# Output product, two norms and the residual of a layer as one stage over three sets of tokens

## The chip, the core and the metric

The kernel runs on one core of a Trainium2 chip. The metric is the device time of one launch in microseconds (us). TensorE (PE in the rows; its weight loads stand as PEld) multiplies, VectorE (DVE) and ScalarE (ACT) do element-wise work, SyncE (SP) issues the transfers. SBUF is the working memory of 128 partitions, PSUM holds eight banks of 512 fp32 columns for the results of TensorE.

## The reference

One step of a four-layer hybrid backbone, on 128 context tokens and 1024 latent tokens (1152 together) of width 1024. The layers' token mixers are RWKV-7, attention, a short convolution, and RWKV-7 again. Around each mixer stands the same frame:

```python
def rmsnorm(x, w):
    x32 = x.astype(jnp.float32)
    y = x32 * lax.rsqrt(jnp.mean(x32 * x32, axis=-1, keepdims=True) + RMS_EPS)
    return (y * w.astype(jnp.float32)).astype(x.dtype)

def sublayer(x, cond, p, i, mixer_fn):
    ada = jax.nn.silu(cond) @ p['w_ada'][i] + p['b_ada'][i]
    shift, scale, gate = jnp.split(ada[:, None, :], 3, axis=-1)
    h = rmsnorm(x, p['norm_pre'][i]) * (1.0 + scale) + shift
    m, extra = mixer_fn(h)
    return x + gate * rmsnorm(m, p['norm_post'][i]), extra
```

The last step of every mixer is a product of its gated result `og` (1152 x 1024) with a 1024 x 1024 weight. That product, the norm of its result `m`, the residual sum, and the norm and shift that make the next layer's `h` are the part that this case is about. It occurs four times; after the last layer there is no next norm and `x` is the output.

## The kernel before

Everything is held transposed: a tensor of 1152 tokens by 1024 channels is 8 blocks (NB) of 128 channels, channels on the partitions, tokens along the free axis. `g.x` holds x, `g.arena` is four such tensors (`g.big[0..3]`), each also named as fp32r (`g.big_r`), the number format in which TensorE takes one pass instead of the two records of a plain fp32 product. To keep fp32 accuracy an fp32 product is made of three fp32r products: a high part of both factors, and two with a low part (factor minus its high part).

The program is a chain of phases. Each phase is one block in which every engine runs its own list of instructions, ordered by semaphores, and ends in a barrier of all engines (`Sems.release`, L146). Per layer: `phase_prenorm`, the mixer's phases, `phase_output`; at the end `phase_end` stores x.

`phase_output` (L2233): SP loads the weight in 8 slabs of 128 x 1024 (512 KB) into two slots (`load_slabs`, L346). VectorE splits slab 0 (`split_slab`: cast L380 into `stage_r`, subtraction L391 in place), then the eight row blocks of `og` (`split_rows`: L380, L399), then slab 1. TensorE makes output block b from slab b: for each of 8 row blocks and 3 products, three chunks of 384 tokens, 72 matmuls (`multiply_split`, L412). Two groups of three PSUM banks alternate. ScalarE copies block b to `m` (L2272) and squares it (L2276), VectorE adds the squares up in `acc` (L2297) and splits slab b+2. Only when all eight blocks are there, TensorE sums over the partitions by a product with ones (L2265), VectorE scales and adds epsilon (L2299), ScalarE takes Ln (L2279) and Exp (L2281), and VectorE multiplies `m` by it (L2302) and adds it to x with the gain (L2229), block by block.

`phase_prenorm` (L288), after a barrier: ScalarE squares x (L311), TensorE sums (L283), VectorE L331, ScalarE Ln and Exp (L314, L316), VectorE multiplies x (L334), ScalarE scales and shifts to h (L320). Before the second RWKV layer SP also stores x to DRAM there.

## Time and profile before

| | us |
|---|---|
| median of 3 runs | 5144.27 (5140.68 to 5149.32) |
| the profiled execution | 5141.56 |
| its span, first to last instruction | 5139.8 |
| mean granted TensorE clock over the span | 0.946 of full |
| busy: PE, DVE, ACT | 4371.9 (85%), 2637.6 (51%), 1976.1 (38%) |
| the new stage's place, after layers 0, 1, 2 | 187.0, 186.4, 184.6 |
| the same after layer 3, with the store of y | 161.9 |

The last two lines are measured from the end of the last VectorE instruction of the mixer's last phase (1624.98, 2758.56, 3361.62, 4977.87 us) to the end of the last ScalarE instruction of the next layer's `phase_prenorm` (1811.94, 2944.92, 3546.21), or to the end of the span. The first prenorm, ahead of layer 0, is not touched. A busy time of TensorE counts overlapping matmuls once and says little on its own. What matters in such a chain of phases is in which stretches TensorE has nothing to do.

### The profile page before, as it was taken

How to read it: one execution, taken by the hardware profiler on the slowest of the kernel's cores; microseconds unless marked ns; L12 is line 12 of the kernel's file. 1: busy time of each engine (PE TensorE's matmuls, PEld its weight loads, DVE VectorE, ACT ScalarE, POOL GpSimd, SP SyncE). 2: the span in 40 equal slices, each digit the busy share in tenths (PEclk: the TensorE clock that was granted, in tenths of full speed). 3: DMA queues.
4: the chain of work that ended last, by engine and by line, in shares of the span. 5: the costliest groups of instructions: out<-in, count | busy, mean ns of one | idle time of the engine just before them, and what ended most of it. 6: DMA issues, size and time to landing. Idle time of an engine off the chain costs nothing. (4 is left out here: it accounts for less than half of the span.)

```text
span 5139.8 us, 135171 instructions
## 1 busy us (share of the span) xinstructions
PE 4371.9 (85%) x60324; PEld 3611.7 (70%) x60324; DVE 2637.6 (51%) x4169; ACT 1976.1 (38%) x3418; POOL 2.7 (0%) x8
## 2 busy tenths in 40 slices
PE   3799988999987689888888599985999989999966
PEld 0488867888874655446667499983888777888846
DVE  0552447777764313145565343336533477777753
ACT  1553225555544223046663300015432245555441
POOL 0000000000000000000000000000000000000000
PEclk7899999999998889989999799997999989999988
DMA  9134593333316010000000011111345843333261
GB/s 417 49 112 128 156 257 114 92 95 93 93 55 164 17 40 29 27 1 1 1 1 26 17 37 45 41 33 62 102 130 157 236 139 94 95 92 90 65 164 57
DMA packets 624902, 465.61 MB, mean 91 GB/s; under 512 B 27488, under 2 KB 600288, under 8 KB 619744
## 3 DMA queue, kind: packets, MB, share of 16 engines
q1 hardware_dynamic: 493536, 391.29, 24.9%
q10 hardware_dynamic: 130816, 66.07, 4.7%
q8 instruction: 458, 7.50, 0.6%
q14 instruction: 92, 0.75, 0.1%
HBM read 333.28 MB, written 123.99 MB: 89 GB/s over the span
## 5 line engine op out<-in xcount | busy, mean ns | idle before, releaser
L412 PE MATMUL ps<-big_r,stage_r 128*128 128x384 f32 x3072 | 625.6, 338 | 86.0 <-DVE big_r L399 85.7
L660 PE MATMUL ps<-big_r,stage_r 128*128 128x384 f32 x2976 | 640.6, 350 | 17.1 <-DVE big_r L891 15.8
L412 PEld LDWEIGHTS ps<-big_r,stage_r 128*128 128x128 f32 x3072 | 545.9, 190 | 94.5 <-issue 85.7
L660 PEld LDWEIGHTS ps<-big_r,stage_r 128*128 128x128 f32 x2976 | 521.8, 189 | 101.2 <-issue 53.6
L412 PE MATMUL ps<-big_r,w_slab_r 128*128 128x384 f32 x1536 | 351.9, 337 | 0.0
L660 PE MATMUL ps<-big_r,w_slab_r 128*128 128x384 f32 x1488 | 340.3, 336 | 0.0
L368 PE MATMUL ps<-arena,w_slab 128*128 128x384 f32 x864 | 295.0, 503 | 27.0 <-DVE arena L1953 24.1
L412 PEld LDWEIGHTS ps<-big_r,w_slab_r 128*128 128x128 f32 x1536 | 277.1, 190 | 0.0
L368 PEld LDWEIGHTS ps<-arena,w_slab 128*128 128x128 f32 x864 | 169.2, 197 | 153.2 <-issue 47.5
L2105 DVE TENSOR_REDUCE extra<-ps 128x1 f32<-128x1152 f32 (+1 forms) x144 | 171.8, 1234 | 200.3 <-PE ps L2017 200.3
L660 PEld LDWEIGHTS ps<-big_r,w_slab_r 128*128 128x128 f32 x1488 | 268.1, 189 | 0.0
L1434 ACT COPY arena<-ps 128x512 f32<-128x512 f32 x288 | 169.1, 587 | 256.7 <-PE ps L1239 256.1
L1588 DVE COPY_PREDICATED arena<-arena,ps 128x128 f32<-128x128 uint32 x720 | 192.9, 325 | 118.6 <-PE ps L1227 117.6
L2085 ACT COPY arena<-ps 128x384 f32<-128x384 f32 (+1 forms) x400 | 175.3, 470 | 197.1 <-PE ps L2035 197.0
L1461 ACT COPY arena<-ps 128x256 f32<-128x256 f32 x360 | 136.5, 379 | 275.9 <-PE ps L1250 225.2
L2035 PE MATMUL ps<-ident,arena 128*128 128x128 f32 x1168 | 189.7, 287 | 51.2 <-DVE arena L2118 23.8
L768 ACT ACTIVATE x_resid<-ps,chan 128x384 f32<-128x384 f32 x192 | 101.2, 579 | 305.6 <-PE ps L694 242.3
L380 DVE CAST stage_r<-w_slab 128x1024 fp32r<-128x1024 f32 x64 | 44.4, 694 | 339.1 <-DMA w_slab<-in_w 328.0
L1227 PE MATMUL ps<-arena 64*64 64x32 f32 x7680 | 166.7, 222 | 57.2 <-ACT arena L1434 49.0
L1239 PE MATMUL ps<-arena 64*64 64x64 f32 x9216 | 202.9, 224 | 9.5 <-issue 5.6
L1192 PE MATMUL ps<-arena 64*128 64x128 f32 x2304 | 172.6, 289 | 43.1 <-DVE arena L1560 29.9
L2035 PEld LDWEIGHTS ps<-ident,arena 128*128 128x128 f32 x1168 | 123.3, 141 | 106.1 <-DVE arena L2112 80.6
(221 smaller groups left out, 7677.4 us busy)
## 6 DMA issues: line engine op xcount, KB each, us to landing
w_slab<-in_w SPq DMA_DIRECT2D x138, 512.0 KB, 3.7
scan_in<-x_resid ACTq DMA_DIRECT2D x112, 576.0 KB, 5.4
arena<-in_w_ada SPq DMA_DIRECT2D x24, 2048.0 KB, 27.6
arena<-scan_in SPq DMA_DIRECT2D x80, 576.0 KB, 7.6
arena<-scan_in SPq DMA_DIRECT2D x144, 320.0 KB, 3.9
arena<-scan_in SPq DMA_DIRECT2D x288, 128.0 KB, 3.9
arena<-scan_in SPq DMA_DIRECT2D x144, 192.0 KB, 4.2
scan_y<-arena SPq DMA_DIRECT2D x144, 128.0 KB, 2.2
```

The lines of the kernel that those rows point to most:

```text
L368: mm = pe.matmul(g.ps[:, bank + c, 0:CW], g.slab[:, slot, k * P:(k + 1) * P], rhs[:, k, c * CW:(c + 1) * CW], start=k == 0, stop=k == NB - 1)
L412: mm = pe.matmul(g.ps[:, bank + c, 0:CW], w[:, k * P:(k + 1) * P], x[:, k, c * CW:(c + 1) * CW], start=k == i == 0, stop=k == NB - 1 and i ...
L660: mm = pe.matmul(g.ps[:, 3 * s + c, 0:CW], w[:, k * P:(k + 1) * P], x[:, k, chunk(c)], start=k == i == 0, stop=k == NB - 1 and i == 2)
L1192: mm = pe.matmul(strided(ps, (3 + h) * 512 + u * P, (1, P)), strided(bk[q % 2], u * 256 + t * P, (1, P), rows=HALVES[h]), strided(ar[q % 4 ...
L1227: mm = pe.matmul(strided(ps, p * 512 + u * 32, (1, 32), rows=HALVES[h]), strided(gr[q % 3], (1 - p) * 1024 + h * 512 + u * P, (1, HD), row ...
L1239: mm = pe.matmul(strided(ps, h * 512 + (2 * d + s) * HD, (1, HD), rows=HALVES[p]), strided(xt[q % 2], lx(d, p, s), (1, HD), rows=HALVES[h] ...
L1434: A.copy(strided(x, 0, (HD, 2), (P, 4), (1, HD)), strided(ps, 0, (512, 2), (HD, 4), (1, HD))).then_inc(xa_ok, 1)
L1461: A.copy(strided(xt[q % 2], n, (256 - n, 2), (2 * n, P // n), (1, n)), src).then_inc(xt_ok, 1)
L1588: V.copy_predicated(strided(wk(k), p * P, (256 + n, 2), (2 * n, HD // n), (1, n)), bits(strided(level_mask, (k - 1) * P, (HD, 2), (n, HD / ...
L2035: mm = pe.transpose(g.ps[:, turned_bank(n, h, k), i * P:(i + 1) * P], prob[n % 2][h][:, (3 * k + i) * P:(3 * k + i + 1) * P], g.ident[:, :])
L2085: A.copy(prob_t[n % 2][h][:, 3 * k * P:3 * k * P + w], g.ps[:, turned_bank(n, h, k), 0:w]).then_inc(tr_ok, 1)
L2105: V.tensor_reduce(nmax[n % 2][h], scored(n, h), mybir.AxisListType.X, ALU.max, negate=True).then_inc(max_ok, 1)
```

## The change

`phase_output`, the following `phase_prenorm` and `phase_end` become one phase, `phase_boundary`. The tokens are taken in three sets of 512, 384 and 256 (`CHUNKS`). A unit (i, b) is output block b for set i: 8 row blocks by 3 products, 24 matmuls as wide as the set, into one of six PSUM banks in turn. Banks 6 and 7 hold the sums of the two norms. The weight's high and low parts are kept for all eight slabs (`w_high`, `w_low`, in the arena), so each slab is loaded and split once, during set 0; ScalarE now casts the high part (`high_slab_of`), VectorE makes the low part (`low_slab_of`). Row blocks are split set by set (`split_row`, order in `ROWS_AT`). What follows a set's last unit, called its tail here, is issued while TensorE works on the next set: `sum1`, `mean1`, `root1` (Ln, Exp) for the norm of m, `residual`, then `square2`, `add2`, `sum2`, `mean2`, `root2` for the norm of x, then `scaled` (VectorE) and `shifted` (ScalarE). `RESIDUAL_AT`, `SQUARE_AT` and `RESULT_AT` say beside which unit of the next set each is issued. The tail of set 2 has nothing beside it. `sq1`, `acc1`, `rstd1` lie in `stage`, `acc2`, `rstd2` in `extra`, `sq2` in `w_slab`. After the last layer the second norm is left out and y is stored set by set; so is x ahead of the second RWKV layer. The convolution's buffers are renumbered so that h is where the stage leaves it, with no other change there.

```diff
+        phase_prenorm(nc, g, layers[0])
         for layer in layers:
             j = layer // 3
-            phase_prenorm(nc, g, layer)
...
-            phase_output(nc, g, layer)
-        phase_end(nc, g)
+            phase_boundary(nc, g, layer, layer == layers[-1])
...
+CHUNKS = ((0, 512), (512, 896), (896, 1152))
+ROWS_AT = ((0, 1, 2), (3,), (), (), (4, 5), (6,), (7,), ())
+RESIDUAL_AT = ((), (0,), (1, 2, 3), (4, 5, 6), (7,), (), (), ())
+SQUARE_AT = ((), (), (0, 1, 2), (3, 4, 5), (6,), (7,), (), ())
+RESULT_AT = ((), (), (0,), (1, 2, 3), (4,), (5,), (6,), (7,))
...
+            for b in range(NB):
+                if b >= WSLOTS:
+                    sp.wait_ge(wl_ok, b - WSLOTS + 1)
+                sp.dma_start(g.slab[:, b % WSLOTS, :], g.io["w"][base + b]).then_inc(slab_in[b % WSLOTS], 16)
+            dest = g.io["y"] if last else g.x_kept[1] if MIXER[layer + 1] == 0 else None
+            if dest is not None:
+                for i in range(LAST + 1):
+                    sp.wait_ge(x_ok, NB * (i + 1))
+                    sp.dma_start(dest[:, :, tokens(i)], g.x[:, :, tokens(i)]).then_inc(x_st, 16)
+                sp.wait_ge(x_st, 16 * (LAST + 1))
...
+            def unit(i, b):
+                u = NB * i + b
+                if i == 0:
+                    pe.wait_ge(wl_ok, b + 1)
+                if u >= 6:
+                    pe.wait_ge(m_ok, u - 5)
+                for k in range(NB):
+                    if b == 0:
+                        pe.wait_ge(row_ok, NB * i + k + 1)
+                    for j, (w, r) in enumerate(((w_high, highs[i % 2][:, k, 0:wide[i]]), (w_high, og_r[:, k, tokens(i)]),
+                                                (w_low, highs[i % 2][:, k, 0:wide[i]]))):
+                        mm = pe.matmul(g.ps[:, bank(i, b), 0:wide[i]], w[:, b, k * P:(k + 1) * P], r,
+                                       start=k == j == 0, stop=k == NB - 1 and j == 2)
+                mm.then_inc(unit_mm, 1)
...
+            def sum2(i):
+                pe.wait_ge(acc2_ok, added(i, NB - 1))
+                if i:
+                    pe.wait_ge(ms2_ok, i)
+                pe.matmul(g.ps[:, 7, 0:wide[i]], g.ones[:, :], part(acc2, i), start=True, stop=True).then_inc(sum2_mm, 1)
+
+            for i in range(LAST + 1):
+                for b in range(NB):
+                    unit(i, b)
+                    if i and b == 0:
+                        sum1(i - 1)
+                    if i and b == 6 and not last:
+                        sum2(i - 1)
...
+            def square1(i, b):
+                u = NB * i + b
+                act.wait_ge(unit_mm, u + 1)
...
+            def result(i, b):
+                if i:
+                    act.wait_ge(x_ok, NB * (i - 1) + b + 1)
+                A.copy(part(m[b], i), g.ps[:, bank(i, b), 0:wide[i]]).then_inc(m_ok, 1)
...
+            high_slab_of(0)
+            high_slab_of(1)
...
+            for i in range(LAST + 1):
+                for b in range(NB):
+                    square1(i, b)
+                    if i == 0:
+                        result(i, b)
+                        if b + 2 < NB:
+                            high_slab_of(b + 2)
+                        continue
+                    for k in RESULT_AT[b]:
+                        result(i, k)
+                    if b == 0:
+                        root1(i - 1)
+                    if last:
+                        continue
+                    for k in SQUARE_AT[b]:
+                        square2(i - 1, k)
+                    if b == 6:
+                        root2(i - 1)
+                    if b == 7 and i < LAST:
+                        for k in range(NB):
+                            shifted(i - 1, k)
+            root1(LAST)
+            if not last:
+                for b in range(NB):
+                    square2(LAST, b)
+                    shifted(LAST - 1, b)
+                root2(LAST)
+                for b in range(NB):
+                    shifted(LAST, b)
...
+            def residual(i, b):
+                if b == 0:
+                    dve.wait_ge(rstd1_ok, i + 1)
+                dve.wait_ge(m_ok, NB * i + b + 1)
+                for c, a0, a1 in pieces(i):
+                    V.scalar_tensor_tensor(part(m[b], i, a0, a1), part(m[b], i, a0, a1), gain(b, c), part(rstd1, i, a0, a1),
+                                           op0=ALU.mult, op1=ALU.mult).then_inc(t_ok, 1)
+                dve.wait_ge(t_ok, t_count(i, b))
+                V.tensor_tensor(g.x[:, b, tokens(i)], part(m[b], i), g.x[:, b, tokens(i)], op=ALU.add).then_inc(x_ok, 1)
...
+            split_row(0, 0)
+            low_slab_of(0)
+            for k in range(1, NB):
+                split_row(0, k)
+            low_slab_of(1)
+            for i in range(LAST + 1):
+                for b in range(NB):
+                    add1(i, b)
+                    if i == 0 and b + 2 < NB:
+                        low_slab_of(b + 2)
+                    if i and b == 0:
+                        mean1(i - 1)
+                    if i < LAST:
+                        for k in ROWS_AT[b]:
+                            split_row(i + 1, k)
+                    if i:
+                        for k in RESIDUAL_AT[b]:
+                            residual(i - 1, k)
+                            if k and not last:
+                                add2(i - 1, k - 1)
+                        if b == 5 and not last:
+                            add2(i - 1, NB - 1)
+                        if b == 6 and not last:
+                            mean2(i - 1)
+                        if b == 7 and i < LAST and not last:
+                            for k in range(NB):
+                                scaled(i - 1, k)
+            mean1(LAST)
+            if not last:
+                for b in range(NB):
+                    scaled(LAST - 1, b)
             for b in range(NB):
-                if b + 2 < NB:
-                    split_slab(nc, g, dve, b + 2, slab_in, proj_done, high_ok, low_ok)
-                dve.wait_ge(sq_ok, b + 1)
-                if b:
-                    dve.wait_ge(acc_ok, b)
-                V.tensor_tensor(acc, acc, sq[b % 2], op=ALU.add).then_inc(acc_ok, 1)
-            dve.wait_ge(sum_mm, 1)
-            V.tensor_scalar(as3(ms), slot_view(g.ps[:, 0:3, :]), 1.0 / D, RMS_EPS, ALU.mult, ALU.add).then_inc(ms_ok, 1)
-            dve.wait_ge(rstd_ok, 1)
-            for b in range(NB):
-                V.tensor_tensor(tmp[:, b, :], m[:, b, :], rstd, op=ALU.mult).then_inc(tmp_ok, 1)
-                if b:
-                    dve.wait_ge(tmp_ok, b)
-                    residual(nc, g, ada, tmp, b - 1, x_ok)
-            dve.wait_ge(tmp_ok, NB)
-            residual(nc, g, ada, tmp, NB - 1, x_ok)
-            dve.wait_ge(x_ok, 2 * NB)
-
-
-def phase_end(nc, g):
-    with ExitStack() as ctx:
-        stored = Sems(nc, ctx)("stored_y")
-        block = ctx.enter_context(nc.Block())
-
-        @block.sync
-        def _(sp):
-            sp.dma_start(g.io["y"], g.x[:, :, :]).then_inc(stored, 16)
-            sp.wait_ge(stored, 16)
-
+                residual(LAST, b)
+            if not last:
+                mean2(LAST)
+                for b in range(NB):
+                    scaled(LAST, b)
```

VectorE, layer 0, the end of the stage. Before, after the last sum of squares the whole width of 1152 tokens is treated at once, and x is written with the gain in one instruction per token group:

```order
L391 TENSOR_TENSOR w_slab_r<-w_slab,stage_r 128x1024
L2297 TENSOR_TENSOR arena<-arena 128x1152 x3
L2299 TENSOR_SCALAR arena<-ps 128x1152
L2302 TENSOR_TENSOR arena<-arena 128x1152 x2
L2229 SCALAR_TENSOR_TENSOR x_resid<-arena,ada,x_resid 128x128
L2229 SCALAR_TENSOR_TENSOR x_resid<-arena,ada,x_resid 128x1024
```

Now, from set 0's `mean2` (L2484) on, at the end of set 1 and the start of set 2: L2450 is `add1`, L2489 `scaled` of set 0, L2454 `mean1` of set 1, L2461 and L2464 the two steps of `residual` of set 1, L2477 `add2`:

```order
L2484 TENSOR_SCALAR extra<-ps 128x512
L2450 TENSOR_TENSOR stage<-stage 128x384
L2489 TENSOR_TENSOR arena<-x_resid,extra 128x512 x8
L2454 TENSOR_SCALAR stage<-ps 128x384
L2450 TENSOR_TENSOR stage<-stage 128x256
L2461 SCALAR_TENSOR_TENSOR arena<-arena,ada,stage 128x384
L2464 TENSOR_TENSOR x_resid<-arena,x_resid 128x384
L2450 TENSOR_TENSOR stage<-stage 128x256
L2461 SCALAR_TENSOR_TENSOR arena<-arena,ada,stage 128x384
L2464 TENSOR_TENSOR x_resid<-arena,x_resid 128x384
```

The tail's instructions of one set have moved between the `add1` of the next. On ScalarE the same place, before, was the end of the stage:

```order
L2272 COPY arena<-ps 128x1152
L2276 ACTIVATE arena<-arena 128x1152
L2279 ACT_TABLE_LOAD
L2279 ACTIVATE arena<-arena 128x1152
L2281 ACT_TABLE_LOAD
L2281 ACTIVATE arena<-arena 128x1152
```

Now, from the last `shifted` of set 0 (L2389) on: L2355 is `square1` of set 2, L2364 and L2366 `root1` of set 1, L2360 `result`, L2378 `square2` of set 1:

```order
L2389 ACTIVATE arena<-arena,ada 128x128
L2389 ACTIVATE arena<-arena,ada 128x384
L2355 ACTIVATE stage<-ps 128x256
L2364 ACT_TABLE_LOAD
L2364 ACTIVATE stage<-stage 128x384
L2366 ACT_TABLE_LOAD
L2366 ACTIVATE stage<-stage 128x384
L2355 ACTIVATE stage<-ps 128x256 x2
L2360 COPY arena<-ps 128x256
L2378 ACTIVATE w_slab<-x_resid 128x384 x3
```

The eight `shifted` of set 0 stand ahead of the first square of set 2, and the function tables of Ln and Exp are loaded in the middle of the sets, ten times a stage where there were four.

## Rows read from the trace of the kernel before

**Rows 1.** Windows: length, busy PE, PEld, DVE, ACT, POOL; clock; DMA share; GB/s.
```profile
1624.98:1634.24 9.26, 0.00 (x0) 0.03 (x1) 4.09 (x6) 0.00 (x0) 0.00 (x0) 0.50 0.32 114
1634.24:1738.16 103.92, 103.58 (x576) 102.30 (x576) 37.40 (x36) 16.02 (x14) 0.00 (x0) 0.97 0.10 31
1738.16:1811.94 73.78, 21.95 (x54) 11.83 (x54) 36.22 (x35) 33.49 (x34) 0.00 (x0) 0.67 0.00 0
2758.56:2944.92 186.36, 125.60 (x630) 114.22 (x630) 77.73 (x76) 49.52 (x48) 0.00 (x0) 0.84 0.07 23
3361.62:3546.21 184.59, 123.04 (x630) 112.26 (x630) 77.70 (x76) 49.52 (x48) 0.00 (x0) 0.84 0.13 49
4977.87:5139.80 161.93, 107.11 (x582) 103.83 (x582) 66.12 (x67) 23.20 (x20) 0.00 (x0) 0.83 0.15 55
```

**Rows 2.** Timeline, VectorE, layer 0: first slab cast; a run of eight like instructions.
```profile
1630.08 0.69 DVE L380 CAST stage_r<-w_slab 128x1024 fp32r<-128x1024 f32 x1 [5.10 <-DMA w_slab<-in_w]
...
1798.30 10.24 DVE L334 TENSOR_TENSOR arena<-x_resid,arena 128x1152 f32<-128x1152 f32 x8 [3.70 <-ACT arena L316]
```

**Rows 3.** Timeline, TensorE, layer 0 (start, us, what, count).
```profile
1637.26 2.12 PE L412 MATMUL ps<-big_r,stage_r 128*128 128x384 f32 x6
1639.18 1.03 PE L412 MATMUL ps<-big_r,w_slab_r 128*128 128x384 f32 x3
...
1700.52 1.20 PE L412 MATMUL ps<-big_r,stage_r 128*128 128x384 f32 x6
1701.56 0.68 PE L412 MATMUL ps<-big_r,w_slab_r 128*128 128x384 f32 x3
```

**Rows 4.** Groups by line and form, ScalarE (count, busy us, mean ns).
```profile
L1461 ACT COPY arena<-ps 128x256 f32<-128x256 f32 x360 | 136.5, 379 | 275.9 <-PE ps L1250 225.2 <-PE ps L1260 50.3
L1430 ACT ACTIVATE arena<-arena 128x512 f32<-128x512 f32 x144 | 82.9, 626 | 0.0
L320 ACT ACTIVATE arena<-arena,ada 128x1024 f32<-128x1024 f32 x32 | 39.2, 1226 | 0.0
L320 ACT ACTIVATE arena<-arena,ada 128x128 f32<-128x128 f32 x32 | 15.4, 481 | 5.7 <-DVE arena L334 5.7
L779 ACT CAST stage_r<-w_slab 128x1024 fp32r<-128x1024 f32 x12 | 12.6, 1046 | 18.0 <-DMA w_slab<-in_w 16.0 <-ACT x_resid L739 2.0
L2279 ACT ACT_TABLE_LOAD x4 | 5.1, 1283 | 0.1
```

**Rows 5.** Groups by line and form, VectorE.
```profile
L391 DVE TENSOR_TENSOR w_slab_r<-w_slab,stage_r 128x1024 fp32r<-128x1024 f32 x64 | 78.5, 1226 | 2.2
L1539 DVE TENSOR_TENSOR arena<-arena 128x512 f32<-128x512 f32 x72 | 49.3, 685 | 0.0
L380 DVE CAST stage_r<-w_slab 128x1024 fp32r<-128x1024 f32 x64 | 44.4, 694 | 339.1 <-DMA w_slab<-in_w 328.0 <-issue 11.1
L2229 DVE SCALAR_TENSOR_TENSOR x_resid<-arena,ada,x_resid 128x1024 f32<-128x1024 f32 x32 | 40.9, 1279 | 0.0
L1612 DVE TENSOR_TENSOR arena<-arena 128x256 f32<-128x256 f32 x72 | 30.6, 425 | 2.5
L380 DVE CAST big_r<-arena 128x1152 fp32r<-128x1152 f32 x40 | 30.1, 753 | 0.0
L2229 DVE SCALAR_TENSOR_TENSOR x_resid<-arena,ada,x_resid 128x128 f32<-128x128 f32 x32 | 11.1, 346 | 0.0
```

**Rows 6.** Timeline, TensorE, attention's phase: plain fp32 products of 256 and 512 columns.
```profile
1829.82 22.61 PE L1862 MATMUL ps<-arena 128*128 128x256 f32 x104
...
1890.24 1.88 PE L1885 MATMUL ps<-arena,extra 128*128 128x512 f32 x4
```

**Rows 7.** Issues of transfers on the page, and the last one's time in the timeline.
```profile
scan_in<-x_resid ACTq DMA_DIRECT2D x112, 576.0 KB, 5.4
...
out_y<-x_resid SPq DMA_DIRECT2D x1, 4608.0 KB, 12.5
...
5126.49 0.35 SPq L2318 DMA_DIRECT2D out_y<-x_resid  x1
```

More of the change, by code:

```diff
@@ L2241, in phase_output @@
-    sq = [work[:, i, :] for i in range(2)]
-    acc = work[:, 5, :]
-    ms, root, rstd = work[:, 2, :], work[:, 3, :], work[:, 4, :]
-    ada = g.ada[:, layer]
-    V, A = nc.vector, nc.scalar
+    n = NB * T
+    w_at, rest_at = (n if og_at == 0 else 0), 3 * n
+    w_high, w_low = g.w_out[w_at]
+    wide = [a1 - a0 for a0, a1 in CHUNKS]
+    at, highs = rest_at, []
+    for k in range(2):
+        size = max(wide[k::2])
+        highs.append(g.big_r[3][:, :, :].rearrange("p b t -> p (b t)")[:, at - rest_at:at - rest_at + NB * size].rearrange("p (b t) -> p b t", b=NB))
+        at += NB * size
@@ new lines, in phase_boundary @@
+    halves = (w_at + 2 * NB * D, at)
+    assert at + 4 * 512 <= 4 * n
+    m = [g.arena[:, halves[b // 4] + b % 4 * 512:halves[b // 4] + (b % 4 + 1) * 512] for b in range(NB)]
+    flat = g.stage[:, :, :].rearrange("p a b -> p (a b)")
+    sq1 = [flat[:, 512 * i:512 * i + 512] for i in range(2)]
+    acc1, rstd1 = flat[:, 1024:1536], flat[:, 1536:2048]
+    acc2, rstd2 = g.extra[:, 0:512], g.extra[:, 512:1024]
+    sq2 = [g.slab[:, i, 0:512] for i in range(2)]
+    gain = lambda b, c: g.ada[:, layer, 16 + b, c:c + 1]
@@ new lines, in phase_boundary, with pieces, part @@
+    V, A = nc.vector, nc.scalar
+    LAST = len(CHUNKS) - 1
+    def pieces(i):
+        return [(c, max(r0, CHUNKS[i][0]), min(r1, CHUNKS[i][1])) for c, r0, r1 in token_ranges()
+                if max(r0, CHUNKS[i][0]) < min(r1, CHUNKS[i][1])]
+    def part(ap, i, a0=None, a1=None):
+        start = CHUNKS[i][0]
+        return ap[:, 0:wide[i]] if a0 is None else ap[:, a0 - start:a1 - start]
+    tokens = lambda i: slice(*CHUNKS[i])
+    t_count = lambda i, b: sum(NB * len(pieces(k)) for k in range(i)) + (b + 1) * len(pieces(i))
@@ new lines, in sum1 @@
+            def sum1(i):
+                pe.wait_ge(acc1_ok, added(i, NB - 1))
+                if i:
+                    pe.wait_ge(ms1_ok, i)
+                pe.matmul(g.ps[:, 6, 0:wide[i]], g.ones[:, :], part(acc1, i), start=True, stop=True).then_inc(sum1_mm, 1)
+            def sum2(i):
[3 more added lines that the diff above has]
+                pe.matmul(g.ps[:, 7, 0:wide[i]], g.ones[:, :], part(acc2, i), start=True, stop=True).then_inc(sum2_mm, 1)
@@ new lines, in _ @@
+            for i in range(LAST + 1):
[5 more added lines that the diff above has]
+                        sum2(i - 1)
+            sum1(LAST)
+            if not last:
+                pe.wait_ge(ms2_ok, LAST)
+                for b in range(NB):
+                    pe.wait_ge(sq2_ok, NB * LAST + b + 1)
+                    pe.matmul(g.ps[:, 7, 0:wide[LAST]], g.ones[:, :], part(sq2[b % 2], LAST), start=b == 0, stop=b == NB - 1).then_inc(last_mm, 1)
@@ L2280, in _, with high_slab_of @@
-            act.wait_ge(root_ok, 1)
-            A.activation(rstd, root, ACT.Exp, scale=-0.5).then_inc(rstd_ok, 1)
+            def high_slab_of(b):
+                act.wait_ge(slab_in[b % WSLOTS], 16 * (b // WSLOTS + 1))
+                A.copy(w_high[:, b, :], g.slab[:, b % WSLOTS, :]).then_inc(wh_ok, 1)
+            def square1(i, b):
+                u = NB * i + b
+                act.wait_ge(unit_mm, u + 1)
+                if b >= 2:
+                    act.wait_ge(acc1_ok, added(i, max(b - 2, 1)))
+                elif i:
+                    act.wait_ge(acc1_ok, added(i - 1, b + NB - 2))
+                A.activation(part(sq1[b % 2], i), g.ps[:, bank(i, b), 0:wide[i]], ACT.Square).then_inc(sq1_ok, 1)
@@ new lines, in result, with root1 @@
+            def result(i, b):
+                if i:
+                    act.wait_ge(x_ok, NB * (i - 1) + b + 1)
+                A.copy(part(m[b], i), g.ps[:, bank(i, b), 0:wide[i]]).then_inc(m_ok, 1)
+            def root1(i):
+                act.wait_ge(ms1_ok, i + 1)
+                A.activation(part(rstd1, i), part(rstd1, i), ACT.Ln).then_inc(ln1_ok, 1)
+                act.wait_ge(ln1_ok, i + 1)
+                A.activation(part(rstd1, i), part(rstd1, i), ACT.Exp, scale=-0.5).then_inc(rstd1_ok, 1)
@@ new lines, in add2 @@
+            def add2(i, b):
+                dve.wait_ge(sq2_ok, NB * i + b + 1)
+                if b == 0:
+                    return
+                if b == 1:
+                    if i:
+                        dve.wait_ge(sum2_mm, i)
+                    first = part(sq2[0], i)
+                else:
+                    dve.wait_ge(acc2_ok, added(i, b - 1))
+                    first = part(acc2, i)
+                V.tensor_tensor(part(acc2, i), first, part(sq2[b % 2], i), op=ALU.add).then_inc(acc2_ok, 1)
```

116 lines of the change are left out of this document (80 added, 36 removed).

## The prediction

> **What bounds the kernel now.** I read the windows first, because the change touches four places of a long chain of phases. Around layer 0's output product the window has three parts [rows 1]: 9.3 us in which TensorE does nothing, 103.9 us of products at 0.97 of the clock, and 73.8 us in which TensorE has 54 short matmuls, while VectorE (36 us) and ScalarE (33 us) take turns. So the product itself is bound by TensorE, and 83 of 187 us are not covered by it. The places after layers 1 and 2 are alike (186.4 and 184.6 us), the last is 161.9 us long and ends with the store of y [rows 1]. The four are 720 us of 5141.56; the rest of the kernel is the same code, and I count it as unchanged.
>
> **What stays.** The number of matmuls stays (8 x 72 = 3 x 8 x 24 = 576), and so do the columns. At full clock six 384-wide fp32r matmuls take 1.04 us, 0.1733 each, that is 384/2.4 = 160 ns and 13 more [rows 3]; at half clock 1.92/6 = 0.320 [rows 3]. No row shows 512 or 256 wide in fp32r. The plain fp32 products bound them from below: 256 columns take 22.61/104 = 0.217 us a record, 512 about 0.43, and such a record passes its columns at half the rate, so 0.108 and 0.215 for a single pass [rows 6]. From above, 256 can cost what 384 does, 0.173, if the weight load sets the pace (the loads stand beside every matmul, busy 102.3 us of the 103.9 [rows 1]), and 512 adds its 13 ns: 0.227. I take column time plus 13 ns: 0.2267, 0.1733, 0.120, since 384 is the nearest row; it is near the lower bound for 256. Units are then 5.44, 4.16 and 2.88 us, 99.8 us for all 24, as 8 x 72 x 0.1733 before.
>
> **A rule on the other side.** The Trainium skill, "TensorE: Matmul & The Clock Gate", section "LDWEIGHTS (loading the stationary operand)", gives a load by its column count alone, 128/1.2 = 107 ns, which would fit under 256 columns and leave no loss. Its section "Back-to-back issue gap" gives N/2.4 + 2.5 ns. The trace disagrees for fp32r: 173 ns, not 162.5, at 384 wide. By that gap the set 0 and set 2 units would be 5.2 and 2.6 us. The sum below uses neither.
>
> **Other durations.** VectorE, fp32, by line through the forms: a sum or product of 512, 384, 256 columns 0.685, 0.555, 0.425; gain times norm (as L2229) of 128, 384, 256: 0.346, 0.61, 0.48; cast of 512 0.46 [rows 5]. ScalarE: square, copy, Ln or Exp 0.38 at 256, some 0.48 at 384, 0.6 at 512; scale and shift 0.48, 0.59, 0.69 at 128, 256, 384; cast of a slab 1.05; a function table 1.28 [rows 4]. Like instructions overlap: eight of 1.353 take 10.24, so about 0.09 less each [rows 2]; a dependent one starts about 0.03 late. This is an estimate for each new width.
>
> **A middle stage, from the end of the mixer.** Set 0: slab 0 is there at 5.1 as before [rows 2]. Row block 0 is split while it flies. Cast on ScalarE 1.05 and low part on VectorE 1.23 give the first matmul at 7.4 (9.3 before). Seven more row blocks at 0.46 + 0.69 less overlap, 1.09 each, reach 15.1, and unit 0 ends at 15.8; TensorE, at half clock for its first 5 to 6 us [rows 1, 3], needs 1.28 per row block there and then catches up. Low slab 1 comes at 16.3. Seven units of 5.44: 54.4. Slab b+2 is ready 0.6 + 0.6 + 1.05 + 1.23 = 3.5 after unit b, hidden under unit b+1 (5.4); with less than 3.5 of cover it would show each time.
>
> Set 1: 8 x 4.16 and two sums over 512 columns in plain fp32, 0.86 each. TensorE reaches `sum2(0)` at 84.2. VectorE has rstd1 at 62.5 and starts `residual(0, 0)` at 65.3; the first takes 1.5, seven blocks of residual and `add2` 2.09 each (14.6), six `add1` 2.8, three row blocks 2.1, waits for the squares 0.8: 87.1. So TensorE waits 2.9 us, and set 1 ends at 92.3.
>
> Set 2: TensorE has its seven units and `sum1(1)` done at 112.9. ScalarE squares and copies unit 7 (93.1), waits for `scaled`, and shifts all of set 0: 8 x (0.39 + 0.60), to 102.0. Queued behind stand the first square of set 2 and `root1(1)` with two table loads: 105.6. On that waits VectorE: from 106.3 eight residuals of 1.1, seven `add2` of 0.47, the `add1` of 0.34 between, to 119.9. `sum2(1)` sits ahead of unit 7 on TensorE, which waits 7.0 us. Then 0.64 and 2.88: 123.6.
>
> Tail of set 2, nothing beside it: square, add, sum, mean 2; eight `scaled` of set 1, 4; eight residuals of 0.85, 6.8, with the squares and ScalarE's `shifted` of set 1 (0.93 a block) ending at 137.7; mean, Ln, table, Exp to 140.8; first `scaled` 0.5, eight shifts of 0.5 to 145.4. The savings are 187.0, 186.4 and 184.6 less 145.4: 41.6, 41.0 and 39.2. The two barriers inside are in them.
>
> **The last stage** has no second norm, so nothing waits: 54.4 + 33.3 + 0.86 = 88.5, + 23.0 + 0.64 = 112.2. Square to Exp 3.9, eight residuals 6.9: 123.0. The store is 1 MB instead of 4.5. Between 576 KB at 5.4 and 4608 KB at 12.5 that is 6.2 us; 0.8 follows as before (5126.49 + 12.5 against 5139.8) [rows 7]. 130.0 against 161.9: 31.9 saved. The store of x before layer 3, 1 MB again, is hidden under mean, root and shifts (9 us); the loads of the next phase wait for the barrier as now.
>
> Sum: 41.6 + 41.0 + 39.2 + 31.9 = 153.7. The profiled execution goes from 5141.56 to 4987.9. The median is 2.7 above the profiled one; I forecast the median, 4990.
>
> **The rivals.** (1) 256-wide matmuls at the weight load's pace, 0.173: unit 4.16 in set 2. In a middle stage six of the units are under the 7 us wait and one shows with some rest, +3.2; in the last +10.2. Together +19.8: 5010. For it: the loads stand as dense as the matmuls. Against: at half clock 384 takes 0.320, no more than its columns, so loads didn't bind there. 0.13. (2) The 7 us wait lets the clock fall: in the window behind the product the granted clock is 0.67 [rows 1]. Unit 7 of set 2 then costs 24 x 0.213 = 5.1 instead of 2.9, the sums behind it double; +3.5 a stage, +10: 5000. 0.13. (3) No 13 ns at other widths, 0.215 and 0.108: 2.1 less in a middle stage, 3.3 in the last, 9.5 in all: 4981. This is the time that the skill's gap rule named above would give. 0.08. (4) The change doesn't do what it says: the in-order queues put each tail on TensorE's path. Sets 0 and 1 have some 20 us of tail each, so a middle stage would be back at 185 and only the last one gain: 5110. Against: 7 us, not 20, is what I find. 0.04. (5) Slower: TensorE's stops keep the granted clock at half through the sets. Then 576 matmuls take 192 x (0.427 + 0.320 + 0.213) = 184 instead of 99.8, four times +84.5 = 338, and 5144 - 154 + 338 = 5328. It decides from 154/338 = 45% of the columns at half. Against: before, with row blocks coming one by one, half clock lasted 5 to 6 us and the window has 0.97 [rows 1]; set 0 has no stop after its first unit. 0.02.
>
> **How the numbers follow.** The forecast has 0.60 and, with 2 to 4 us of error a stage from the widths without a row, its own range is 4976 to 5004. The range that leaves out less than 2 in 10 goes from rival 3 less that error, 4970, to rival 1 plus some of it, 5018. A difference of 0.2% (10 us) is what a measurement of this kernel can tell from none. Faster 0.97, same 0.01, slower 0.02.
>
> **What would show it.** First matmul 7.4 us after the mixer, unit 0's end at 16. Matmul starts 227, 173, 120 ns apart. TensorE idle for about 3 us ahead of `sum2` in set 1, released by `add2`, and 7 us in set 2; none in the last stage. ScalarE in one piece of 8 us of `shifted` at the start of set 2. 22 us from the last unit to the last shift. The middle stages 145, the last 130. Wrong would be: 173 ns at 256 wide; a granted clock of half inside the sets; unit ends of set 0 more than 5.5 us apart, which would mean the slab path is not hidden; or other phases that change their length.

## The result, and the profile after

The changed kernel takes 5010.66 us (median of 4 runs, 5006.82 to 5015.15), the kernel before, beside it, 5146.55 (5140.68 to 5149.32): a ratio of 0.9738, 95% interval 0.9721 to 0.9755. Forecast were 4990 and a range of 4970 to 5018, so the range holds it and the forecast is 20.7 us too low. The profiled execution took 5006.82 us with a span of 5005.0.

The four places, windows as in [rows 1] (the columns are the same):

```profile
1634.03:1784.60 150.57, 118.30 (x602) 102.44 (x602) 89.92 (x178) 77.38 (x136) 0.00 (x0) 0.86 0.09 29
2730.46:2880.21 149.75, 118.46 (x602) 102.69 (x602) 89.94 (x178) 77.38 (x136) 0.00 (x0) 0.88 0.09 29
3295.99:3444.75 148.76, 117.08 (x602) 102.17 (x602) 89.92 (x177) 77.39 (x136) 0.00 (x0) 0.89 0.18 61
4876.75:5005.00 128.25, 105.31 (x582) 95.06 (x582) 69.78 (x136) 39.41 (x68) 0.00 (x0) 0.90 0.20 70
```

150.6, 149.8, 148.8 and 128.3 us stand against 187.0, 186.4, 184.6 and 161.9 before: 36.4, 36.6, 35.8 and 33.6 saved, 142.4 in all, where the forecast had 153.7. The rest of the span, which the change leaves alone, is 4427.7 us against 4420.0. Layer 0's stage cut into its sets, by windows again:

```profile
1634.03:1650.00 15.97, 8.32 (x24) 5.72 (x24) 10.63 (x19) 2.11 (x3) 0.00 (x0) 0.63 0.29 99
1650.00:1688.50 38.50, 38.39 (x169) 31.81 (x170) 18.20 (x29) 13.17 (x20) 0.00 (x0) 1.00 0.22 69
1688.50:1728.10 39.60, 36.84 (x198) 35.00 (x198) 26.17 (x56) 19.20 (x33) 0.00 (x0) 0.96 0.00 0
1728.10:1762.50 34.40, 27.11 (x196) 25.82 (x194) 20.57 (x40) 24.03 (x48) 0.00 (x0) 0.85 0.01 1
1762.50:1784.60 22.10, 7.65 (x18) 4.08 (x18) 14.35 (x35) 18.87 (x34) 0.00 (x0) 0.64 0.00 0
```

Set 0 behind its first unit is TensorE alone: 38.39 of 38.50 us, 169 matmuls, 0.228 each. VectorE works 26 us and ScalarE 19 in set 1, where before they had 36 and 33 us behind the product [rows 1]. So the tails are covered. But set 2 has 7.3 us without TensorE and a granted clock of 0.85. TensorE's timeline shows where (start, us, line, what, first shape, count; in brackets the idle time ahead and what ended it; a row can run over from one unit's shape to the next's):

```profile
1641.53 8.41 PE L2312 MATMUL ps<-big_r,w_out 128*128 128x512 f32 x24 [15.14 <-DVE w_out L2429]
1650.11 42.57 PE L2312 MATMUL ps<-big_r,w_out 128*128 128x512 f32 x192 [0.17 <-DVE w_out L2429]
...
1721.27 2.07 PE L2326 MATMUL ps<-extra,ones 128*128 128x512 f32 x2 [2.77 <-DVE extra L2477]
1722.35 8.55 PE L2312 MATMUL ps<-big_r,w_out 128*128 128x384 f32 x48
1730.75 0.81 PE L2320 MATMUL ps<-stage,ones 128*128 128x384 f32 x2
1731.10 17.72 PE L2312 MATMUL ps<-big_r,w_out 128*128 128x256 f32 x144
1756.11 1.65 PE L2326 MATMUL ps<-extra,ones 128*128 128x384 f32 x2 [7.29 <-DVE extra L2477]
1756.98 5.52 PE L2312 MATMUL ps<-big_r,w_out 128*128 128x256 f32 x24
1763.43 0.70 PE L2320 MATMUL ps<-stage,ones 128*128 128x256 f32 x2 [0.94 <-DVE stage L2450]
```

L2326 is `sum2`. Both waits stand where the prediction put them, 2.77 and 7.29 us long (2.9 and 7.0 forecast), and both are ended by `add2` (L2477). What the prediction had not taken into its sum is behind them, in windows of TensorE (length, busy and count, clock, DMA share, GB/s):

```profile
1718.50:1721.30 2.80, 0.04 (x2) 0.94 0.00 0
1721.30:1724.30 3.00, 3.00 (x6) 0.50 0.00 0
1724.30:1727.70 3.40, 3.40 (x21) 0.99 0.00 0
...
1748.80:1756.10 7.30, 0.02 (x1) 0.70 0.01 2
1756.10:1762.20 6.10, 6.09 (x25) 0.52 0.01 3
```

Behind the 2.8 us stop the granted clock is 0.50, the 1.2 GHz level, for about 3 us; behind the 7.3 us stop it is 0.52 over all of unit (2, 7). That unit's 24 matmuls take 5.52 us in the timeline. At full clock they take 3.32 (below). In layer 2 the half clock ended inside that unit, whose first and last starts are 4.23 us apart instead of 5.24; this is why the stage there is 1.0 us shorter than in layer 1.

### The profile page after: what moved, and what is told of

Read it like the earlier page. It is cut to its first block and busy times, and to the rows that moved or that the text cites. A ratio compares the mean times of both kernels' runs of the same rounds, so it can differ in the third digit from the quotient of the medians.

```text
span 5005.0 us, 135676 instructions
## 1 busy us (share of the span) xinstructions
PE 4352.7 (87%) x60240; PEld 3573.9 (71%) x60240; DVE 2677.8 (54%) x4545; ACT 2075.3 (41%) x3730; POOL 2.7 (0%) x8
## 5 line engine op out<-in xcount | busy, mean ns | idle before, releaser
L663 PE MATMUL ps<-big_r,stage_r 128*128 128x384 f32 x2976 | 642.8, 351 | 16.9 <-DVE big_r L894 15.5
L663 PEld LDWEIGHTS ps<-big_r,stage_r 128*128 128x128 f32 x2976 | 524.0, 190 | 100.9 <-issue 54.1
L2312 PE MATMUL ps<-big_r,w_out 128*128 128x512 f32 (+2 forms) x2304 | 428.6, 348 | 47.8 <-DVE w_out L2429 47.6
L2312 PEld LDWEIGHTS ps<-big_r,w_out 128*128 128x128 f32 x2304 | 385.0, 196 | 92.8 <-DVE w_out L2429 51.1
L663 PE MATMUL ps<-big_r,w_slab_r 128*128 128x384 f32 x1488 | 340.9, 336 | 0.0
L415 PE MATMUL ps<-big_r,stage_r 128*128 128x384 f32 x1536 | 309.1, 335 | 17.1 <-DVE big_r L402 17.0
L415 PEld LDWEIGHTS ps<-big_r,stage_r 128*128 128x128 f32 x1536 | 270.5, 188 | 19.1 <-issue 16.6
L663 PEld LDWEIGHTS ps<-big_r,w_slab_r 128*128 128x128 f32 x1488 | 268.5, 189 | 0.0
L2038 PEld LDWEIGHTS ps<-ident,arena 128*128 128x128 f32 x1168 | 123.6, 141 | 105.9 <-DVE arena L2115 80.3
L1195 PEld LDWEIGHTS ps<-arena 64*128 64x128 f32 x2304 | 144.8, 192 | 73.1 <-issue 47.8
```

The costliest lines, as they stand in the source:

```text
L415: mm = pe.matmul(g.ps[:, bank + c, 0:CW], w[:, k * P:(k + 1) * P], x[:, k, c * CW:(c + 1) * CW], start=k == i == 0, stop=k == NB - 1 and i ...
L663: mm = pe.matmul(g.ps[:, 3 * s + c, 0:CW], w[:, k * P:(k + 1) * P], x[:, k, chunk(c)], start=k == i == 0, stop=k == NB - 1 and i == 2)
L1195: mm = pe.matmul(strided(ps, (3 + h) * 512 + u * P, (1, P)), strided(bk[q % 2], u * 256 + t * P, (1, P), rows=HALVES[h]), strided(ar[q % 4 ...
L2038: mm = pe.transpose(g.ps[:, turned_bank(n, h, k), i * P:(i + 1) * P], prob[n % 2][h][:, (3 * k + i) * P:(3 * k + i + 1) * P], g.ident[:, :])
L2312: mm = pe.matmul(g.ps[:, bank(i, b), 0:wide[i]], w[:, b, k * P:(k + 1) * P], r, start=k == j == 0, stop=k == NB - 1 and j == 2)
```

## The experiments

Each kernel is the changed one with one edit. "Stage" is measured as in the table of before, in the profiled execution; "outside" is the span less the four stages.

| kernel | median us | ratio to before (95%) | middle stages | last | outside |
|---|---|---|---|---|---|
| before | 5146.55 | | 187.0, 186.4, 184.6 | 161.9 | 4420.0 |
| the change | 5010.66 | 0.9738 (0.9721 to 0.9755) | 150.6, 149.8, 148.8 | 128.3 | 4427.7 |
| before again | 5146.61 | 0.9998 (0.9988 to 1.0008) | 186.9, 186.2, 187.3 | 161.3 | 4424.5 |
| the change again | 5016.68 | 0.9732 (0.9706 to 0.9758) | 150.7, 149.8, 148.7 | 128.4 | 4432.0 |
| busy_wait | 4997.65 | 0.9698 (0.9676 to 0.972) | 146.4, 145.8, 145.9 | 128.6 | 4426.4 |
| sum2_late | 5000.82 | 0.9705 (0.9686 to 0.9725) | 147.9, 146.9, 147.1 | 128.5 | 4421.3 |
| shift_spread | 4998.05 | 0.9694 (0.9673 to 0.9715) | 144.2, 145.1, 143.3 | 128.4 | 4437.9 |
| serial_tails | 5188.12 | 1.0077 (1.0055 to 1.01) | 199.7, 199.0, 198.5 | 164.8 | 4420.9 |
| equal_sets | 4977.8 | 0.9665 (0.9647 to 0.9683) | 140.0, 139.3, 138.8 | 132.8 | 4425.9 |
| sets_448 | 4975.77 | 0.9667 (0.965 to 0.9683) | 140.9, 140.5, 140.3 | 128.3 | 4424.1 |
| equal_middle | 4974.41 | 0.9656 (0.9642 to 0.9669) | 139.9, 139.2, 138.8 | 129.1 | 4433.7 |
| equal_spread | 4971.43 | 0.9661 (0.9648 to 0.9675) | 140.4, 139.7, 139.9 | 128.4 | 4419.7 |

The ratio is that of the runs taken side by side. The stages of the change hardly move between its two executions (150.6 and 150.7), one place of before moves by 2.7 us (184.6 and 187.3), and the outside moves by up to 18 us over the twelve.

**The change again.** The same kernel, to see what repeats.

> The changed kernel once more, unedited: how far the phases that the change doesn't touch move from one execution to the next. Theory A (the 7.8 us that the changed kernel's execution has outside the four new stages, most of it before the first of them, is spread between executions): the stages come again at 150.6, 149.8, 148.8 and 128.3 us within 1, the phases ahead of the first one at 1634.0 within 10 us either way, by the clock that is granted there. Rival (the new program slows the other phases): 1634 within 1 us again, and the total 5007 to 5015.

The stages came back within 0.2 us each. The first began at 1631.6 instead of 1634.0, more than the 1 us that the rival allows, and the outside was 4.3 us longer. So the stages of the change are solid, the saving in them is 142 us (144 against the second execution of before, further down), and the kernel's time carries some us of spread that has nothing to do with them.

**Waits filled with products (busy_wait).** My theory is that the missing 5 us a middle stage are the clock behind the two waits. The rival is that the chain of VectorE and ScalarE is longer than I worked out. The edit puts products ahead of both `sum2`, as many as the wait is long, whose results `sum2` overwrites:

```diff
+            def busy(i, n):
+                if i:
+                    pe.wait_ge(ms2_ok, i)
+                for _ in range(n):
+                    pe.matmul(g.ps[:, 7, 0:256], w_high[:, 0, 0:P], highs[1][:, 0, 0:256] if i == 0 else highs[0][:, 0, 0:256], start=True, stop=True)
...
             def sum2(i):
+                busy(i, (20, 56)[i])
                 pe.wait_ge(acc2_ok, added(i, NB - 1))
```

> Ahead of each sum2 TensorE is kept at work by products of 256 columns into the free bank 7, 20 in set 1 and 56 in set 2 (2.4 and 6.7 us, inside the waits of 2.9 and 7.4). Theory (the 5 us that a middle stage took over the forecast are the clock's, lost behind the two waits): the unit behind each wait runs at full clock, 4.2 and 2.9 us in place of 5.4 and 5.3, and a middle stage falls from 150 to about 146; 12 us in all, ratio to the changed kernel 0.9976. Rival (they are late VectorE and ScalarE work, and the clock costs nothing because TensorE is not what ends the stage): a middle stage stays at 150.

TensorE's timeline of busy_wait (L2326 are the added products, L2333 is `sum2`) and two of its windows:

```profile
1712.49 2.55 PE L2326 MATMUL ps<-big_r,w_out 128*128 128x256 f32 x20
1715.43 1.13 PE L2333 MATMUL ps<-extra,ones 128*128 128x512 f32 x2 [0.40 <-DVE extra L2484]
1715.99 7.60 PE L2312 MATMUL ps<-big_r,w_out 128*128 128x384 f32 x48
...
1741.34 6.88 PE L2326 MATMUL ps<-big_r,w_out 128*128 128x256 f32 x56
1748.81 0.91 PE L2333 MATMUL ps<-extra,ones 128*128 128x384 f32 x2 [0.59 <-DVE extra L2484]
1749.26 3.32 PE L2312 MATMUL ps<-big_r,w_out 128*128 128x256 f32 x24
```

```profile
1716.00:1718.50 2.50, 2.50 (x15) 1.00 0.00 0
...
1748.80:1752.40 3.60, 3.59 (x26) 1.00 0.00 0
```

76 products more and a stage 4.1, 4.0 and 2.8 us shorter (4 each were expected). The clock stays at 1.00, the last unit takes 3.32 instead of 5.52 and the sums half. The stop in set 1 is part of it: unit (1, 7) has its last start 92.12 us after the mixer instead of 93.68, and `sum2(1)` comes at 120.54 instead of 122.08.

The first matmul doesn't fall alike in all stages (7.50, 6.53 and 6.62 us after the mixer in the change). Counted from it, the three stages of busy_wait are 139.0 us each, those of the change 143.1, 143.2 and 142.1, and the forecast of 145.4 less 7.4 is 138.0. So the clock theory stands, with 4.1, 4.2 and 3.1 us, and 1.0 is left in each stage for the other engines.

**The second sum behind unit 7 (sum2_late).** This asks what sets the end once TensorE isn't held back: with `sum2` behind unit 7, TensorE does the unit first and waits after it.

```diff
-                    if i and b == 6 and not last:
+                    if i and b == 7 and not last:
                         sum2(i - 1)
```

> sum2 of the set before is issued behind unit 7 in place of behind unit 6. TensorE no longer waits in set 1 (unit 7 ends at 88.5, not 93.7) and in set 2 waits only when its products are done. Theory (the end of a middle stage is set by the chain of ScalarE and VectorE, the place of sum2 on TensorE matters only through the clock): a middle stage 145 to 147, since no unit runs at half clock behind a wait; the last stage unchanged at 128.3. Rival (TensorE's place of the wait is the bound): set 2 ends 9 us earlier and the stage falls by nearly as much, to 141 to 142.

The stages are 147.9, 146.9 and 147.1, near the 145 to 147 of the chain theory and far from 141 to 142. `sum2(1)` now stands alone, with the last unit done ahead of it:

```profile
1748.02 1.65 PE L2326 MATMUL ps<-extra,ones 128*128 128x384 f32 x2 [5.15 <-DVE extra L2477]
```

It starts at 120.79 us, about where busy_wait has it (120.54). The end hangs on when VectorE has its sums, whichever side of it the last unit stands. So the 7 us wait was not there to be won on TensorE.

**The shifts spread out (shift_spread).** Which link of the chain in set 2 can be shortened? ScalarE's block of shifts stands at its start, ahead of `root1(1)`; in the changed kernel, its timeline:

```profile
1729.80 7.99 ACT L2389 ACTIVATE arena<-arena,ada 128x128 f32<-128x128 f32 x16 [0.86 <-DVE arena L2489]
1737.69 0.36 ACT L2355 ACTIVATE stage<-ps 128x256 f32<-128x256 f32 x1
1738.07 1.28 ACT L2364 ACT_TABLE_LOAD   x1
```

The edit issues one row block's shift behind each unit of set 2 instead:

```diff
-                    if b == 7 and i < LAST:
-                        for k in range(NB):
-                            shifted(i - 1, k)
+                    if i == LAST and b:
+                        shifted(0, b - 1)
+                    if i == LAST and b == 7:
+                        shifted(0, 7)
```

> The eight shifted of set 0, one block of 8 us on ScalarE ahead of set 2's first square, are issued one behind each unit of set 2. Theory (that block is what makes sum2 of set 1 late): root1 of set 1 comes 8 us earlier, TensorE's wait in set 2 falls from 7.4 to 3 to 4 us, a middle stage to 147 to 148. Rival (the chain from residual to add2 on VectorE is the bound by its own length): the wait falls by less than 1 us and the stage stays at 150.

```profile
1722.25 1.13 PE L2326 MATMUL ps<-extra,ones 128*128 128x512 f32 x2 [2.78 <-DVE extra L2478]
...
1751.37 1.65 PE L2326 MATMUL ps<-extra,ones 128*128 128x384 f32 x2 [3.04 <-DVE extra L2478]
1752.24 4.39 PE L2312 MATMUL ps<-big_r,w_out 128*128 128x256 f32 x24
```

In layer 0 `sum2(1)` comes at 116.25 instead of 122.08, 5.8 us earlier, and the stages are 6.4, 4.7 and 5.4 us shorter, more than expected. Not all of that is the shifts'. In layers 0 and 2 the clock stayed at 1.00 behind the first stop (2.78 us), where it fell in the changed kernel (windows at the end of this text); unit (1, 7) has its last start at 92.09, as in busy_wait. In layer 1 it fell as in the changed kernel:

```profile
2809.45 2.07 PE L2326 MATMUL ps<-extra,ones 128*128 128x512 f32 x2 [2.78 <-DVE extra L2478]
2810.53 8.65 PE L2312 MATMUL ps<-big_r,w_out 128*128 128x384 f32 x48
```

Counted from the first matmul, `sum2(1)` is 4.2 us earlier there and 5.7 and 5.8 in the other two, so 4.2 us are the shifts' and the other 1.5 the clock's. The wait fell to 3.04, as expected, but the root came only 6.5 us earlier in layer 0, not 8, because its Ln now waits for VectorE's mean:

```profile
1733.99 0.52 ACT L2364 ACTIVATE stage<-stage 128x384 f32<-128x384 f32 x1 [1.85 <-DVE stage L2455]
```

The outside was the longest of all in that execution, 4437.9, which hides part of the gain in the span. So the head of the chain, ScalarE's 8 us, was on the path.

**Before again.** The kernel before as a kernel of its own, to see how far the outside moves by itself.

> The kernel before once more, unedited, for the spread of the phases outside the four places. Three executions of the new kernels have reached the first of the four between 1627.2 and 1635.1 us, the one of before at 1625.0. Theory A (spread between executions, most of it in the scan): before comes anywhere in 1624 to 1636, and its four places again at 187.0, 186.4, 184.6 and 161.9 within 1. Rival (the new program is slower there): again 1625 within 1.

Ratio 0.9998, and an outside of 4424.5 against 4420.0. The first place begins at 1626.7, which fits theory A and is only 0.7 us outside what the rival allows, so this run alone doesn't decide between them. Its last middle stage is 187.3 here and 184.6 in the profiled execution of before: [rows 1] is at the short end there by up to 3 us.

**The tails in series (serial_tails).** All that the change does but one thing: each set's tail is finished before the next set's products. The edit moves calls and makes TensorE wait for the end of each tail (the two `wait_ge`); TensorE's part of it:

```diff
                 for b in range(NB):
                     unit(i, b)
-                    if i and b == 0:
-                        sum1(i - 1)
-                    if i and b == 6 and not last:
-                        sum2(i - 1)
+                if i < LAST:
+                    sum1(i)
+                    if last:
+                        pe.wait_ge(x_ok, NB * (i + 1))
+                    else:
+                        sum2(i)
+                        pe.wait_ge(h_ok, t_count(i, NB - 1))
```

> The same stage, sets, slabs and instructions, but each set's tail is done before TensorE begins the next set, so that the gain of laying them beside it is taken away alone. Theory (the gain is the cover of the tails; the merged phase without it gives none): tails of 38, 29 and 21 us stand in the open, starts of sets 1 and 2 at half clock cost 2 to 3 each, a middle stage is about 204, the last about 166, the whole 5205, slower than before. Rival (the gain comes from the barriers gone, the slabs resident and the first unit's earlier start): it stays faster than before, under 5120.

```profile
1684.49 1.13 PE L2320 MATMUL ps<-stage,ones 128*128 128x512 f32 x2 [1.41 <-DVE stage L2445]
1705.67 2.08 PE L2326 MATMUL ps<-extra,ones 128*128 128x512 f32 x2 [20.05 <-DVE extra L2472]
1719.86 20.44 PE L2312 MATMUL ps<-big_r,w_out 128*128 128x384 f32 x101 [12.12 <-ACT arena L2392]
```

199 us a middle stage, longer than the 187 of before, and 5188.12 us (two executions): 0.8% slower than before. Three sets without cover cost some 13 us a stage (204 was expected); the cover gives 49 back (199.7 less 150.6), its higher granted clock included (0.86 over the stage against 0.78). The last stage is 164.8, 2.9 longer than before. TensorE stands still for 20.05 and 12.12 us in one tail, where the changed kernel has 2.77. Without the overlap nothing of the gain is left.

**Three sets of 384 (equal_sets).** The 7 us wait is there because the tail of 384 tokens has only 256 tokens' products to hide under. With equal sets each has the same cover, and only the bare tail at the end grows.

```diff
-CHUNKS = ((0, 512), (512, 896), (896, 1152))
+CHUNKS = ((0, 384), (384, 768), (768, 1152))
```

> Three sets of 384. The work of set 0's tail on VectorE and ScalarE shrinks by a quarter, and set 2 gives 33 us of cover for the tail of set 1 in place of 23. Theory (the queues of VectorE and ScalarE in sets 1 and 2 are what makes TensorE wait): waits ahead of sum2 under 1 us in both sets, no half clock behind them, the open tail of set 2 longer by 3.5 us; a middle stage 139 to 141, the last stage 130 to 131 in place of 128.3: 4978 to 4985 where the changed kernel gives 5007 to 5015. Rival (the sizes matter little, the chain has its length whatever they are): the waits come back in the longer tail, a middle stage 147 to 150.

```profile
1699.41 0.91 PE L2326 MATMUL ps<-extra,ones 128*128 128x384 f32 x2 [0.56 <-DVE extra L2477]
1699.86 8.78 PE L2312 MATMUL ps<-big_r,w_out 128*128 128x384 f32 x48
...
1734.09 0.81 PE L2326 MATMUL ps<-extra,ones 128*128 128x384 f32 x2
1734.44 4.62 PE L2312 MATMUL ps<-big_r,w_out 128*128 128x384 f32 x24
```

The waits are 0.56 us and none, the clock behind them is full, and the middle stages are 9.9 to 10.6 us shorter than the changed kernel's. The last one is 4.5 longer, 132.8 where 130 to 131 was expected: nothing waits there in either, and the last set with its store is bigger. Counted from the first matmul, which came 0.7 us later here, it is 3.8 longer.

**Sizes between (sets_448).** 448, 384 and 320 in the middle stages, with the shifts spread, and 512, 384, 256 in the last. Beside the line shown, the edit is that of shift_spread.

```diff
+    CHUNKS = ((0, 512), (512, 896), (896, 1152)) if last else ((0, 448), (448, 832), (832, 1152))
```

> Middle stages by sets of 448, 384 and 320 with set 0's shifted one behind each unit of set 2; the last stage with the sizes of the change, 512, 384, 256, for which nothing waits there. By the same durations a middle stage is 139 to 141 and the last 128.3, 4975 to 4982, ratio to before about 0.967; if the sizes matter little it equals the kernel with shifted alone spread, 144.

140.9, 140.5, 140.3 and 128.3, as expected: the last stage as it was, the middle ones 0.9 to 1.4 us over equal sets. TensorE's wait in set 1 is 1.66 us here, with the clock at 1.00 behind it, and there is none in set 2.

**The best sizes for each stage (equal_middle), and the same with the shifts spread (equal_spread).** The line shown is the whole edit of the first; the second adds that of shift_spread.

```diff
+    CHUNKS = ((0, 512), (512, 896), (896, 1152)) if last else ((0, 384), (384, 768), (768, 1152))
```

> Three sets of 384 in the three middle stages, 512, 384 and 256 in the last. The stages are independent of each other, so each should keep the length that it had where its sets were alike: middle 139 to 140 us (equal sets showed 139.99, 139.31, 138.84), last 128.3 to 128.5 (it was 132.81 with equal sets, whose last store is larger). Against equal sets in all four places that is 4.4 us less: 4970 to 4976. If the sizes of the last stage don't matter, it stays at 4977.8.

> As equal_middle, and the shifts of set 0 stand one behind each unit of set 2 instead of all eight ahead of it. The theory that the shifts matter only because sum2(1) waits for the chain behind them expects little here, since with equal sets sum2(1) is reached only about when it is ready: 138 to 140 us a middle stage, at most 1.5 us less than equal_middle. The rival, that the shifts also hold back ScalarE's part of the tail after the last unit, expects 3 us or more a stage, as with 512, 384 and 256, where the spread was worth 5 to 6.5.

139.9, 139.2 and 138.8 for the first, as expected; its last stage, 129.1, is 0.6 us over the 128.3 to 128.5 expected, because the first matmul came at 7.40 us instead of 6.60. With equal sets the spread buys nothing (140.4, 139.7, 139.9, up to 1.1 us longer), where it gave 4.7 to 6.4 with falling sizes, the clock's part included: the block of shifts cost something only through the wait of `sum2(1)`. The three last kernels can't be told apart by their times (4971 to 4976, with intervals that overlap), nor from equal_sets at 4977.8; all are 33 to 39 us under the change.

## Why the prediction was right, and what it missed

**The structure was right.** In layer 0: first matmul 7.50 us after the mixer (7.4 forecast), the last start of unit (0, 0) at 15.51 (end 15.8), that of set 0 at 54.08 (end 54.4), `sum2(0)` at 87.24 (87.1), the shifts of set 0 one piece of 7.99 us (8), a wait of 7.29 (7.0). In layers 1 and 2 the first matmul came at 6.53 and 6.62, which one sum for all three stages had missed. Serial_tails shows that rival (4), tails on TensorE's path, would have given 199 a stage, worse than its 185, and that it isn't what happens here. Rival (5), half clock through the sets, falls with 1.00 in set 0.

**The widths were right.** From one start to the next the matmuls stand 0.227, 0.173 and 0.120 us apart (medians over a unit), the values chosen for 512, 384 and 256. So rival (1), 0.173 at 256 wide, and rival (3), no 13 ns at the other widths, both fall. The last stage, which has no second norm, shows the sum of them with nothing in between: the last unit has its last start 111.1 us after the mixer, where its end was forecast at 112.2. Counted from the first matmul, at 6.60 instead of 7.4, the difference is 0.2. `sum1(2)` follows at 112.3 (4989.06 less 4876.75), when VectorE has its sum.

```profile
4967.53 20.60 PE L2312 MATMUL ps<-big_r,w_out 128*128 128x256 f32 x168
4989.06 0.70 PE L2320 MATMUL ps<-stage,ones 128*128 128x256 f32 x2 [0.94 <-DVE stage L2450]
```

The Trainium skill, "TensorE: Matmul & The Clock Gate", section "Back-to-back issue gap", gives N/2.4 + 2.5 ns for the gap of a matmul by itself: 216, 163 and 109 ns. The trace has 11 ns more at each of the three widths, in fp32r.

**The mis-sized term: the clock behind the waits.** The step is "`sum2(1)` sits ahead of unit 7 on TensorE, which waits 7.0 us. Then 0.64 and 2.88: 123.6." The 2.88 is a unit at full clock; it ran at half, in layer 2 for its first part. Rival (2) had named this with +3.5 a stage and 0.13, and the sum had left it out, though the window behind the product of before, with its 0.67 [rows 1], spoke for it. Rival (2) also applied it to the long wait only. The wait of 2.77 us in set 1 cost as well: unit (1, 7) has its last start at 93.68, against an end of 92.3 forecast. Through the square of that unit, VectorE's `scaled`, ScalarE's queue and `root1(1)` this lateness reaches `sum2(1)`.

Busy_wait, where the clock stays full, splits the 5.2 us between the forecast 145.4 and the 150.6 of layer 0:

- 1.5 from the clock behind the stop in set 1 (`sum2(1)` at 122.08 against 120.54).
- 2.6 from the clock behind the stop in set 2 (from the start of `sum2(1)` to the last start of unit (2, 7) 6.11 us against 3.49).
- 0.6 from the chain to `sum2(1)` (120.54 against 119.9). Most of it stands in ScalarE's queue: in busy_wait the shifts end at 102.2 (102.0 forecast) and `root1(1)`, behind a square and two table loads, at 106.2 (105.6). (A middle stage has twelve table loads, not the ten named with the change.)
- 0.6 from the tail of set 2, 22.4 us in both kernels behind the last start, 21.8 allowed.
- Less 0.2, since the recorded 119.9 + 0.64 + 2.88 is 123.4 and not 123.6.

The other sums of the prediction come out within 0.2 us a term, but for rival (3): by its own spacings the last stage is 4.3 us less, not 3.3, which changes nothing.

**The last stage** was forecast at 130.0 and took 128.3. The products were 1.0 us earlier than forecast and the way from them to the last residual 0.6 longer, so the residuals end at 122.6 (123.0). The store is issued at 4999.39, 5.6 us ahead of the end of the span, where 6.2 + 0.8 = 7.0 had been allowed.

**The rest of the kernel.** "The rest of the kernel is the same code, and I count it as unchanged": it came out 7.7 us longer in the profiled execution. Over the twelve profiled executions it lies between 4419.7 and 4437.9 us, and the kernels with the changed stage are at both ends of that. Most of it arises ahead of the first changed line: the first stage begins between 1625.0 and 1636.9 us, its scan phase takes 782.7 to 795.7 us with the same instructions. Both executions of before are at the low end (1625.0 and 1626.7), those of the change at 1634.0 and 1631.6, but equal_spread and equal_sets, whose code up to there is that of the change, start at 1625.2. I take it for spread between executions. What causes it stays open.

**The sum again.** The profiled execution was to take 4987.9 and took 5006.82, 18.9 more: 11.3 are stages (153.7 less 142.4) and 7.7 the unchanged phases. The median lies 3.8 above the profiled execution instead of 2.7, and 0.6 went in rounding 4990.6 to 4990; that is the 20.7. With rival (2) as the forecast it would have been 5000, and the stage 148.9.

**That the range held is partly luck.** 5010.66 lies outside the 4976 to 5004 that the prediction gives its own forecast. It lies inside 4970 to 5018, whose upper end was set by rival (1), and the 0.120 us at 256 columns refutes that rival. What moved the result was the clock of rival (2), priced at 3.5 us a stage and worth 4.1, 4.2 and 3.1, and the unchanged phases, which no rival had.

**What the change left.** The profile of a covered tail says what to size: the tail of a set must fit under the products of the next set. Falling sizes give the smallest bare tail at the end (22.4 us behind the last unit) and the least cover for the tail before it. In layer 0 equal sets have the last start of the last unit 113.5 us after the mixer instead of 128.2 and 26.5 us of bare tail behind it, 4.1 more, so they are better in the three stages with both norms; in the last, where the second norm is missing, nothing waits, and the small last set is better.

## What to carry to other kernels

When work is taken in sets so that the element-wise tail of one hides under the products of the next, work out for each pair whether the tail fits, and choose the sizes by that before making the last set small. Price a wait of TensorE as the wait plus what comes behind it: here 7 us of waiting cost 2.6 us more in the sum and the 24 matmuls behind it, and a wait of 2.8 us could cost 1.5. And look at an in-order queue for a block of work that nobody needs yet (the shifts) ahead of one that everybody waits for (the root).
